# Projecting the context's first keys and values inside the first mixture of a transformer kernel, with a new order for the second stage

## Chip, cores and metric

The kernel runs on one core of a Trainium2 chip, in float32. The metric is the device time of one execution in microseconds (us); of several executions the median is taken. TensorE is called PE, VectorE DVE, ScalarE ACT, GpSimd POOL, SyncE SP, as in the profile.

## The reference, cut to what matters

Two blocks are applied to x (256 tokens of width 1024).

```python
x = x + token_mixer(rmsnorm(x))                # first block: 8 + 8 heads, forgetting and dilated attention
x = x + hierarchical_moe(rmsnorm(x))           # 32 experts, 1024 -> 512 -> 1024, two of them for each token
# second block, layer 0
h, hc = modulate(x, ...), modulate(ctx, ...)   # shifts, scales, gates: silu(c) @ ada_w, silu(c_ctx) @ ada_w
q, k, v, f = split(h @ attn_w_in)              # q, k, v of width 768, f of width 256
kc, vc = split(hc @ attn_w_in[:, 768:2304])    # keys and values of 256 context tokens
y = concat(diff_attend(q, [k, kc], [v, vc]), fourier_mix(f)) @ attn_w_out   # 6 differential heads
x = x + g_m * y
x = x + g_f * ec_moe(modulate(x, ...))         # 16 experts, 1024 -> 1024 -> 1024, 32 tokens for each expert
# layer 1: a gated short convolution in the place of attention, then a second ec_moe
```

Keys and queries are normalized for each head, multiplied by a gain, and turned by rope, but the context's keys get no rope. The context (hc, kc, vc) does not depend on x.

## The kernel before

**The ring.** All weights come through a ring of six slots of 2 MB (SLOTS = 6). plan_items lists the items in the order in which SP loads them. Before it issues item i, SP waits until item i - 6 has been released (load, free_main); it issues in order. A projection's item is released by its last matmul, a mixture's by M.done, a conditioning half ("ada") by its last addition. Two items of each mixture (LENT = 4 and 7) go into borrowed memory instead (arena from HEAD on, and gate_rows).

**The stages.** Stage 1 is norm, six projections with 16 attention heads in two token tiles between them, and the output projection; then routing (route1_dve, rank_pe) and the first mixture M1 with 32 experts. For each expert expert_pe does gate (L1461), turns the earlier expert's activation, up (L1461), the sums of four partial results (L1480), down of the expert before (L1511), and adds it back to the tokens (back_pe, L1537). For every fourth expert the tokens of four experts are gathered (L1379). Items of expert e in M1 are 3e - 1 (gate), 3e (up), 3e + 1 (down of e - 1). PE, ACT and DVE write out experts 0 to 3 and 28 to 31 and loop three times over eight experts; SP has a loop too. Then more_passes branches: only when an expert has more than 32 tokens is the whole mixture run again. close_y_pe (L1543) closes the sums.

**Stage 2** (block2_pe, block2_act, block2_dve, block2_pool) walks one list, steps2(), on every engine. A unit is one 128-token tile times 512 (wide) or 256 (narrow) columns of weights: projected on PE (proj_pe, L474), squared on ACT (L494), summed on DVE (L506), its root taken on POOL (L262), scaled and multiplied by the gain on DVE (L526, L532), with rope also by a rotation on POOL (L556) and an addition on DVE (L568), turned on PE (L586) and copied by ACT (L596). Values only need a copy. There are 18 units: context and own keys (4), queries (2), own and context values (4), the rest of queries and keys (2), of the context's keys (2), of the context's values and the own values (4). Between them stand attend2(s), the pipelined steps of 12 heads (scores L1952, maximum L1959, exponential L1967, mix L1976 to L1979, turn L1987, values L2012), and the conditioning: ada_add (L378, L384: DVE adds one eighth of a section of ada_w, weighted by silu(c)), ada_sum on PE (L397 to L404) and ada_use on DVE (L415 to L432). The context is normalized and turned in experts 28 to 30 of M1.

**Stage 3** is the convolution with its projections; the second and third mixtures follow the same scheme (16 experts, L1467 and L1511).

Of the kernel before, what the change touches and what calls it, by code (L numbers as in the profile page):

```python
# [9 lines left out]
ALU = mybir.AluOpType  # L10
# [21 lines left out]
LENT = (4, 7)  # L32
LAM_INIT = 0.8 - 0.6


class Mixture:
# [4 lines left out]
    def __init__(self, steps, ne, nf, nd, arrived, done, first, done0, k0, scale, shift, gate, fresh, stage):  # L41
        self.stage, self.lent = stage, LENT if stage else ()
        self.ne, self.nf, self.nd, self.per = ne, nf, nd, 2 * nf + nd
# [65 lines left out]
JOBS = [(s, c) for s in range(12) for c in range(2 if s < 2 else 1)]  # L109
ADDS = [(s, c, k) for s in range(12) for half in range(2) for c in range(2 if s < 2 else 1) for k in range(4 * half, 4 * half + 4)]  # L110
W_IN_COLS = {"qa": 0, "ka": 512, "va": 1024, "qb": 1536, "kb": 2048, "vb": 2560}
CHUNKS1 = ["qb", "kb", "vb", "qa", "ka", "va"]


def plan_items():
# [11 lines left out]
    after = [[], [(0, 0)], [], [(0, 1)], [(1, 0)], [(1, 1)]]  # L127
# [30 lines left out]
def transformer_blocks(nc, x, ctx_in, w_in, w_out, w_gate, w_up, w_down, ada_w, ada_b, attn_w_in, attn_w_out,  # L158
# [3 lines left out]
    with stack:  # L162
# [61 lines left out]
        for i in range(len(items)):  # L224
# [3 lines left out]
            if items[i][0] not in ("ada", "w_in", "attn_w_in", "attn_qk45", "w_out", "attn_w_out", "conv_w_out") or i == ITEM["proj2", 4]:  # L228
# [9 lines left out]
        chain_at = {"dve": 0, "act": 0, "pool": 0}  # L238
# [25 lines left out]
        def pool_step(ins):  # L264
            chain_at["pool"] += 1
            ins.then_inc(pool_chain, 1)
            nc.gpsimd.wait_ge(pool_chain, chain_at["pool"])

# [10 lines left out]
        def norm_act(j, src, i, ready):  # L279
# [6 lines left out]
            nc.scalar.activation(xn[:, 0, :], src[:, 0, :], ACT.Square, accum_out=ss[:, 0:1]).then_inc(sq_done[0], 1)  # L286
# [3 lines left out]
        def norm_dve(j, src, i, ready):  # L290
# [6 lines left out]
            nc.vector.tensor_tensor_reduce(out=xn[:, 1, :], in0=src[:, 1, :], in1=src[:, 1, :], scale=1.0, scalar=0.0,  # L297
# [4 lines left out]
        def norm_pool(j):  # L302

            for t in range(T):
                nc.gpsimd.wait_ge(sq_done[t], j + 1)
                pool_step(nc.gpsimd.tensor_scalar(ss[:, t:t + 1], ss[:, t:t + 1], 1.0 / D, EPS, ALU.mult, ALU.add))
# [51 lines left out]
        accs = {"own": ada_acc[:, :], "ctx": gate_rows[:, 1, 0, :], "even": arena[:, 10240:10240 + D], "odd": arena[:, HEAD:HEAD + D]}  # L358
        acc_of = ["own", "ctx", "own", "ctx", "even", "own", "even", "own", "even", "own", "odd", "own", "odd", "own"]
# [47 lines left out]
        def ada_use_dve(j, banks):  # L407
# [9 lines left out]
            if sec == G_M:  # L417
                g = gate_rows[:, l, 0, :]
# [17 lines left out]
        def heads(name, units, sq, qn, tmp, first_ready, banks):  # L436
# [152 lines left out]
            def put_act(u):  # L589
# [5 lines left out]
                for a, m, dst in un["put"]:  # L595
# [4 lines left out]
                        rope_dve=rope_dve, tr_pe=tr_heads_pe, put_act=put_act, put=put_, vput=vput, added=added,  # L600
# [266 lines left out]
        def turn_out1_pe(g):  # L867
# [4 lines left out]
            pe.wait_ge(ada_used, 2 if br else 4)  # L872
# [26 lines left out]
        def out1_pe(br, t, n):  # L899
# [6 lines left out]
            if br:  # L906
                for s_, v in h1["done"]:
                    pe.wait_ge(s_, v)
                if t:
                    pe.wait_ge(*((at_m, len(att1)) if n else (ada_used, 4)))  # L910
# [14 lines left out]
        CTX = E1 - 3  # L925
# [7 lines left out]
        def ctx_square_act():  # L933
            nc.scalar.wait_ge(ctx_loaded, 32)
            for t in range(T):
                nc.scalar.activation(ctx_junk, ctx_rows[t], ACT.Square, accum_out=ctx_ss[:, t:t + 1]).then_inc(ctx_sq, 1)
                nc.scalar.wait_ge(ctx_sq, t + 1)

        def ctx_root_pool():
            nc.gpsimd.wait_ge(ctx_sq, 2)  # L940
            pool_step(nc.gpsimd.tensor_scalar(ctx_ss, ctx_ss, 1.0 / D, EPS, ALU.mult, ALU.add))
# [7 lines left out]
        def ctx_turn_pe(t):  # L949
# [3 lines left out]
            pe.wait_ge(M1.act, CTX + t + 1)  # L953
# [14 lines left out]
        def ctx_put_dve(t):  # L968
            nc.vector.wait_ge(ctx_tr, 2 * t + 2)
            for k in range(4, KD):  # L970
# [6 lines left out]
                  22: [("ada_sum", 2)], 23: [("ada_use", 2), ("ada_sum", 3)], 24: [("ada_use", 3)],  # L977
# [3 lines left out]
        def attend1(s):  # L981
# [12 lines left out]
            if 18 <= s < 22:  # L994
                yield "ada_add", 1

        def steps1():
# [12 lines left out]
            for u in range(6, 12):  # L1010
# [16 lines left out]
                if u >= 10:  # L1027
# [1518 lines left out]
```

## Time and profile before

| | us |
|---|---|
| median of 3 runs (2025.22 to 2026.14) | 2025.56 |
| the profiled execution | 2021.36 |
| its span, first to last instruction | 2019.5 |
| PE busy | 1496.5 (74%) |
| DVE busy | 485.2 (24%) |
| ACT busy | 246.0 (12%) |
| POOL busy | 89.1 (4%) |
| bytes moved by DMA | 710.94 MB, 352 GB/s on average |

The span in 40 equal slices, busy share in tenths (9 is 90% or more; PEclk is the granted TensorE clock in tenths of full speed):

```text
PE   7999687777767698896765756655997766656665
DVE  3763321111111267743000000001653000000000
PEclk9989799989898899997887888778797887888778
DMA  9532599999999966445999999999893999999997
```

Rows of the windows view give for a stretch the busy us of each engine with the number of instructions, the granted clock (1.00 is 2.4 GHz), the DMA engines' mean busy share and GB/s. Rows of the timeline give start, length, engine, line of the kernel, operation, written and read names, shapes and the number of instructions merged; a bracket at the end gives the idle time of the engine before it and what ended it. A float32 matmul of the program shows as two MATMUL records.

### The profile page before, as it was taken

How to read it: one execution, taken by the hardware profiler on the slowest of the kernel's cores; microseconds unless marked ns; L12 is line 12 of the kernel's file. 1: busy time of each engine (PE TensorE's matmuls, PEld its weight loads, DVE VectorE, ACT ScalarE, POOL GpSimd, SP SyncE). 2: the span in 40 equal slices, each digit the busy share in tenths (PEclk: the TensorE clock that was granted, in tenths of full speed). 3: DMA queues.
4: the chain of work that ended last, by engine and by line, in shares of the span. 5: the costliest groups of instructions: out<-in, count | busy, mean ns of one | idle time of the engine just before them, and what ended most of it. 6: DMA issues, size and time to landing. Idle time of an engine off the chain costs nothing.

```text
span 2019.5 us, 28556 instructions
## 1 busy us (share of the span) xinstructions
PE 1496.5 (74%) x12460; PEld 838.8 (42%) x12460; DVE 485.2 (24%) x965; ACT 246.0 (12%) x603; POOL 89.1 (4%) x102
## 2 busy tenths in 40 slices
PE   7999687777767698896765756655997766656665
PEld 3455444433324344665432424222875432424222
DVE  3763321111111267743000000001653000000000
ACT  2122211111112111332000000001001000000000
POOL 2210000000000042100000000000000000000000
PEclk9989799989898899997887888787997887888778
DMA  9532599999999966445999999999893999999997
GB/s 360 194 140 74 219 405 423 420 422 423 420 423 421 406 252 237 188 163 198 426 419 419 422 421 419 422 421 403 339 372 127 418 419 422 421 420 420 422 420 321
DMA packets 118479, 710.94 MB, mean 352 GB/s; under 512 B 5856, under 2 KB 8416, under 8 KB 93664
## 3 DMA queue, kind: packets, MB, share of 16 engines
q1 hardware_dynamic: 117232, 706.95, 86.0%
q10 hardware_dynamic: 1136, 2.36, 0.3%
q8 instruction: 87, 1.43, 0.3%
q14 instruction: 24, 0.20, 0.0%
HBM read 708.25 MB, written 1.05 MB: 351 GB/s over the span
## 4 chain that ended last, share of the span: by engine, by line
DMA 55%; PE 31%; DVE 7%; issue 4%; POOL 2%; ACT 2%; SPq 0%; DVEq 0%; POOLq 0%; ACTq 0%
DMA ring<-in_moe_w_down 27%; DMA ring<-in_w_down 17%; DMA ring<-in_moe_w_up 11%; PE bank L1511 5%; PE bank L2309 4%; PE bank L474 4%; PE bank L1467 3%; PE bank L1379 3%; PE bank L914 1%; PE bank L618 1%; PE bank L2091 1%; POOL small L262 1%; PE bank L1461 1%; PE bank L1537 1%; DVE ada_acc L378 1%
## 5 line engine op out<-in xcount | busy, mean ns | idle before, releaser
L1467 PE MATMUL bank<-ring,arena 128*32 128x256 f32 x3968 | 286.7, 442 | 160.9 <-DMA ring<-in_moe_w_up 95.0
L1511 PE MATMUL bank<-ring,arena 128*32 128x256 f32 x3008 | 249.9, 490 | 186.6 <-DMA ring<-in_moe_w_down 140.9
L1467 PEld LDWEIGHTS bank<-ring,arena 128*32 128x32 f32 x3968 | 143.9, 123 | 285.2 <-issue 111.6
L1511 PEld LDWEIGHTS bank<-ring,arena 128*32 128x32 f32 x3008 | 119.7, 135 | 304.2 <-issue 193.7
L1461 PE MATMUL bank<-ring,arena 128*32 128x512 f32 x1024 | 136.2, 653 | 56.6 <-DMA ring<-in_w_up 36.8
L474 PE MATMUL bank<-ring,hT 128*128 128x512 f32 (+1 forms) x352 | 157.4, 599 | 1.6 <-DVE hT L336 1.6
L1583 DVE TENSOR_TENSOR arena<-arena,bank 128x128 f32<-128x128 f32 (+1 forms) x64 | 22.7, 355 | 499.0 <-PE bank L1467 496.7
L1379 PE MATMUL bank<-arena,xn 128*128 128x128 f32 x512 | 126.6, 410 | 3.3 <-DVE arena L1411 3.3
L1379 PEld LDWEIGHTS bank<-arena,xn 128*128 128x128 f32 x512 | 123.6, 336 | 8.0 <-issue 4.3
L1537 PE MATMUL bank<-arena 32*128 32x256 f32 x1024 | 95.7, 444 | 16.8 <-PE bank L1537 10.6
L474 PEld LDWEIGHTS bank<-ring,hT 128*128 128x128 f32 x352 | 67.7, 198 | 73.6 <-issue 70.8
L1589 ACT ACTIVATE arena<-bank 128x256 f32<-128x256 f32 x64 | 24.5, 383 | 549.8 <-PE bank L1524 546.7
L1598 DVE TENSOR_TENSOR arena<-bank,gate_strips 128x256 f32<-128x256 f32 x32 | 13.6, 425 | 308.8 <-PE bank L1511 308.8
L2309 PE MATMUL bank<-hT,ring 128*128 128x256 f32 x384 | 85.7, 386 | 1.5 <-ACT hT L328 1.5
L2309 PEld LDWEIGHTS bank<-hT,ring 128*128 128x128 f32 x384 | 74.4, 194 | 12.5 <-ACT hT L328 1.9
L1461 PEld LDWEIGHTS bank<-ring,arena 128*32 128x32 f32 x1024 | 29.9, 115 | 115.3 <-issue 90.5
L1558 DVE COPY arena<-bank 128x512 f32<-128x512 f32 x32 | 22.1, 691 | 211.6 <-PE bank L1461 211.6
L1537 PEld LDWEIGHTS bank<-arena 32*128 32x128 f32 x1024 | 41.8, 191 | 60.8 <-PE bank L1537 37.6
L378 DVE SCALAR_TENSOR_TENSOR ada_acc<-ring,condT,ada_acc 128x1024 f32<-128x1024 f32 x49 | 64.6, 1319 | 1.2
L262 POOL TENSOR_TENSOR small<-small,columns 128x8 f32<-128x8 f32 (+3 forms) x26 | 38.9, 1496 | 294.5 <-DVE small L252 220.2
L1565 ACT ACTIVATE arena<-bank 128x128 f32<-128x128 f32 (+1 forms) x64 | 21.0, 328 | 249.5 <-PE bank L1491 249.5
L1577 ACT ACTIVATE arena<-bank 128x128 f32<-128x128 f32 (+1 forms) x64 | 21.0, 328 | 240.0 <-PE bank L1480 233.2
(263 smaller groups left out, 1289.9 us busy)
## 6 DMA issues: line engine op xcount, KB each, us to landing
ring<-in_moe_w_down SPq DMA_DIRECT2D x64, 2048.0 KB, 26.5
ring<-in_moe_w_gate SPq DMA_DIRECT2D x62, 2048.0 KB, 24.8
ring<-in_moe_w_up SPq DMA_DIRECT2D x62, 2048.0 KB, 26.9
ring<-in_w_gate SPq DMA_DIRECT2D x32, 2048.0 KB, 25.2
ring<-in_w_up SPq DMA_DIRECT2D x32, 2048.0 KB, 26.1
ring<-in_w_down SPq DMA_DIRECT2D x30, 2048.0 KB, 26.5
ring<-in_ada_w SPq DMA_DIRECT2D x24, 2048.0 KB, 13.0
ring<-in_w_in SPq DMA_DIRECT2D x6, 2048.0 KB, 14.6
```

Of the source, the lines that this page charges most:

```text
L262: nc.gpsimd.tensor_tensor(dst, src, minus_half[:, 0:src.shape[1]], ALU.pow).then_inc(roots_done, 1)
L378: ins = dve.scalar_tensor_tensor(acc, w, by, acc, ALU.mult, ALU.add)
L474: last = nc.tensor.matmul(banks[u % NB][:, 0:n], un["lhs"][:, k, :], ring[un["item"] % SLOTS][:, k, a:a + n], start=(k == 0), stop=(k == K ...
L1379: last = nc.tensor.matmul(XG[kk % 4][:, 0:GE * C], xn[:, t, kk::KD], sel[:, b * T + t, :], start=(t == 0), stop=(t == T - 1))
L1461: last = nc.tensor.matmul(GU[up][32 * j:32 * j + 32, :], xgT[:, x + kk, a:a + C], w[:, kk, :], start=(kk < 4), stop=(kk >= 4))
L1467: last = nc.tensor.matmul(GU[up][32 * j:32 * j + 32, 0:QW], xgT[:, x + kk, a:a + C], w[:, kq, j * QW:(j + 1) * QW], start=(kk == 0), stop= ...
L1511: last = nc.tensor.matmul(z_bank(M)[32 * j:32 * j + 32, 0:QW], act_s[:, b, q * C:(q + 1) * C], w[:, kq, j * QW:(j + 1) * QW], start=(kk == ...
L1537: nc.tensor.matmul(Y[2 * t + j // 2][:, at:at + QW], wselT[rows_, e % 2, t * P:(t + 1) * P], z_s[rows_, :], start=(n == 0 and e == 0 and M ...
L1558: v.tensor_copy(up_s, GU[1][:, :]).then_inc(M.u_dve, 1)
L1583: nc.vector.tensor_tensor(silu_s[:, 0:M.w], silu_s[:, 0:M.w], gate_up(M)[1], ALU.mult).then_inc(M.act, 1)
L1589: nc.scalar.activation(wselT[:, e % 2, :], WT[:, 0:S], ACT.Copy).then_inc(M.wT, 1)
L2309: last = nc.tensor.matmul(odd_banks(i)[b // 2][:, (b % 2) * S:(b % 2 + 1) * S], ring[it % SLOTS][:, k, b * P:(b + 1) * P], hT[:, k, :], st ...
```

## The change

What it does, part by part:

1. **Guests.** The context's keys and values of the first four heads (columns 768 to 1279 and 1536 to 2047 of attn_w_in) are projected in M1, at the end of PE's steps of experts 24 and 28 (unit_pe). Their weights are two more items of the ring, placed ahead of the gate item of expert 24 (item 71) and of expert 28 (item 83). Squares, sums, roots, gains and transpositions of the two key tiles follow in experts 24 to 27. The context is loaded in expert 20 and turned in experts 21 and 23. The results stay in the upper arena (k_ctx) and in gate_rows (v_ctx).
2. **Loops.** PE, ACT and DVE loop twice instead of three times over eight experts and write out experts 20 to 31. SP writes out all experts.
3. **Stage 2** has 14 units: context keys and values of heads 4 and 5 first (a new item attn_45, columns 512 to 767 of keys and of values), then own keys, queries, values, the rest. Attention starts at unit 9, with two steps in each of units 9 to 11. The additions are spread anew. x is turned at units 2 and 3.
4. **Conditioning.** Section 3 moves from stage 2 to stage 1, with its two items, eight additions, its sum and its use.
5. **The branch** after M1 is written as a compare-and-branch with a hint, whose place is marked ahead of expert 28.
6. **Routing and norms.** In the first routing the ranking matmuls need only the two choices, not the gates, and the flag for more passes is computed after the first gather. In the other two routings one step is folded into a copy and a fill is moved ahead of a wait. In the norms the scale 1/D goes into the squaring instruction, and the added eps too for the second tile.
7. **Lending.** In stage 2 the first borrowed area is free when the last scores are done.

The diff, cut to its core:

```diff
+CTX_LOAD, CTX_TURN, UNITS, UNIT_TURN = 20, {21: 0, 23: 1}, {24: 0, 28: 1}, {25: 0, 27: 1}
+GUESTS = {3 * e - 1: g for e, g in UNITS.items()}
+SECTIONS = [0, 1, 3, 2, 4, 5, 6, 7, 8, 9, 10, 11]
-    after = [[], [(0, 0)], [], [(0, 1)], [(1, 0)], [(1, 1)]]
+    after = [[], [(0, 0)], [], [(0, 1)], [(1, 0), (1, 1)], [(3, 0), (3, 1)]]
-    items += [("moe", i) for i in range(3 * E1) if i not in LENT]
-    after = [[(2, 0), (2, 1)], [(3, 0)], [(3, 1), (4, 0), (4, 1), (5, 0)], [(5, 1), (6, 0), (6, 1)], [(7, 0), (7, 1)]]
-    for n, item in enumerate([("attn_w_in", 768), ("attn_w_in", 0), ("attn_w_in", 1536), ("attn_qk45",), ("attn_w_in", 2048)]):
+    for i in range(3 * E1):
+        if i in GUESTS:
+            at["guest", GUESTS[i]] = len(items)
+            items.append(("attn_w_in", (768, 1536)[GUESTS[i]]))
+        if i not in LENT:
+            items.append(("moe", i))
+    after = [[], [(2, 0)], [(2, 1), (4, 0)], [(4, 1)], [(5, 0), (5, 1)], [(6, 0), (6, 1), (7, 0), (7, 1)]]
+    for n, item in enumerate([("attn_45", 1), ("attn_w_in", 768), ("attn_w_in", 0), ("attn_w_in", 1536), ("attn_45", 0), ("attn_w_in", 2048)]):
...
+            released[ITEM["guest", g]] = (cu_mm, T * g + T)
+        def unit_pe(n, e):
+            pe.wait_ge(ctx_act, n % T + 1)
+            pe.wait_ge(ctx_dve, n % T + 1)
+            if n % T:
+                pe.wait_ge(M1.act, e + 1)
+            i = ITEM["guest", n // T]
+            wait_item(pe, i)
+            for k in range(KD):
+                last = nc.tensor.matmul(CT[t][:, :], ctxT[:, k, t * P:(t + 1) * P], ring[i % SLOTS][:, k, :], start=(k == 0), stop=(k == KD - 1))
+            last.then_inc(cu_mm, 1)
...
             if e:
                 back_pe(M, k, e - 1, r)
...
+            if M is M1 and e in UNITS:
+                for n in range(T):
+                    unit_pe(T * UNITS[e] + n, e)
+            if M is M1 and e in UNIT_TURN:
+                unit_turn_pe(UNIT_TURN[e], e)
...
             def put(i, rows_):
+                if i in M.guests:
+                    load_one(ITEM["guest", M.guests[i]])
                 free(M, k, i, r, looped)
...
-        LOOPS = E1 // (2 * GE) - 1
+        LOOPS = E1 // (2 * GE) - 2
...
-        def more_passes(eng, passes, one_pass, at_end=None):
-            with eng.If(passes > 0):
+        def more_passes(eng, passes, hint, one_pass, at_end=None):
+            name = f"more_passes_{eng.engine.name}"
+            eng.br_lt(passes, 1, on_true=name + "_none", on_false=name).branch_hint(hint)
...
-        for name, n, ctx in (("k", 0, 1), ("k", 0, 0), ("q", 1, 0), ("v", 2, 0), ("v", 2, 1), ("qk45", 3, 0), ("k45", 3, 1), ("v45", 4, 1),
-                             ("v45", 4, 0)):
+        for name, n, ctx in (("k45", 0, 1), ("v45", 0, 1), ("k", 1, 0), ("q", 2, 0), ("v", 3, 0), ("qk45", 4, 0), ("v45", 5, 0)):
...
-            for u in range(NU2):
+            for u in range(8):
+                yield "proj", (u, (0, 1))
+                if u == 7:
+                    yield "ada_sum", 5
+                if 2 <= u < 4:
+                    yield "turn_x", u - 2
+                yield "sum", u
+                if u == 7:
+                    yield "ada_use", 5
+                if u >= 2:
+                    yield "ada_add", 1
+                if u == 3:
+                    yield "lambda", 0
+                yield "rope", u - 1
+                yield "gain", u
+                if u >= 3:
+                    yield "ada_add", 1
+                if u >= 2:
+                    yield "tr", u - 2
+            for u in range(8, 14):
                 wide = u < 12
+                s = 2 * (u - 9) if wide else u - 6
                 yield "proj", (u, (0,) if wide else (0, 1))
+                if u in (9, 11):
+                    yield "ada_sum", u // 2 + 2
+                    yield "ada_use", u // 2 + 2
+                if u == 8:
+                    yield "tr", 6
+                yield "rope", u - 1
+                yield "tr", u - 1
+                if u > 8:
+                    yield from attend2(s)
+                yield "ada_add", 2 if wide else 1
                 if wide:
                     yield "proj", (u, (1,))
                 yield "sum", u
+                yield "ada_add", 1 if wide else 2
                 yield "gain", u
+                if wide and u > 8:
+                    yield from attend2(s + 1)
+                if wide:
+                    yield "ada_add", 2 if u == 8 else 1
             yield "fourier_proj", 0
+            yield "ada_sum", 8
+            yield "ada_use", 8
             yield from attend2(8)
-            yield "ada_add", 2
+            yield "ada_add", 3
             yield "fourier_proj", 1
             yield from attend2(9)
+            yield "ada_add", 3
             yield "fourier_first", 0
             yield "ada_sum", 9
```

## Rows read from the trace of the kernel before

**Rows 1.** Windows by stage: stage 1, first mixture, stage 2.

```profile
core 0: us, PE busy (x) PEld busy (x) DVE busy (x) ACT busy (x) POOL busy (x), PEclk, DMA share, GB/s
0.00:212.00 212.00, 187.78 (x634) 99.04 (x634) 111.31 (x241) 52.73 (x133) 31.96 (x34) 0.94 0.54 199
...
241.00:694.00 453.00, 343.95 (x3392) 175.08 (x3392) 70.90 (x153) 66.81 (x171) 2.46 (x12) 0.92 1.01 418
694.00:922.00 228.00, 199.34 (x741) 114.67 (x741) 144.84 (x231) 55.70 (x126) 50.39 (x46) 0.96 0.58 222
```

**Rows 2.** Chain of waits in order of time (start, us, what), first mixture, expert 24.

```profile
578.19 26.42 DMA ring<-in_w_down
```

**Rows 3.** Timeline of PE, first mixture, experts 24 and 25.

```profile
574.94 3.20 PE L1511 MATMUL bank<-ring,arena 128*32 128x256 f32 x32 [2.96 <-DMA ring<-in_w_down]
...
579.64 0.71 PE L1537 MATMUL bank<-arena 32*128 32x256 f32 x8 [0.17 <-PE bank L1537]
...
589.85 1.93 PE L1511 MATMUL bank<-ring,arena 128*32 128x256 f32 x32 [1.48 <-DMA ring<-in_w_down]
```

**Rows 4.** Transfers: L1724 from 110 to 215 us; the page's DMA issues.

```profile
DMA to landing us min/median/max: 7.7/7.8/9.1
...
ring<-in_w_down SPq DMA_DIRECT2D x30, 2048.0 KB, 26.5
```

**Rows 5.** Timeline of PE, stage 2: wide unit, transpositions, two narrow units' time.

```profile
712.63 7.03 PE L474 MATMUL bank<-ring,gate_rows 128*128 128x512 f32 x16
...
726.37 0.60 PE L586 MATMUL bank<-cb,arena 128*128 128x128 f32 x4
...
815.78 3.62 PE L474 MATMUL bank<-ring,gate_rows 128*128 128x256 f32 x16
```

**Rows 6.** Timeline of PE at the branch.

```profile
699.31 1.87 PE L1543 MATMUL bank<-columns 128*128 128x1 f32 x8 [5.51 <-issue]
701.04 8.50 PE L474 MATMUL bank<-ring,gate_rows 128*128 128x512 f32 x16
```

**Rows 7.** Timeline of PE, stage 2: the long gaps, the last conditioning sum.

```profile
752.78 0.66 PE L586 MATMUL bank<-cb,arena 128*128 128x128 f32 x4 [2.62 <-DVE gate_rows L421]
...
804.31 1.09 PE L586 MATMUL bank<-cb,arena 128*128 128x128 f32 x4 [5.77 <-issue]
...
830.76 0.69 PE L586 MATMUL bank<-cb,arena 128*128 128x128 f32 x2 [5.95 <-DVE gate_strips L415]
...
869.46 1.05 PE L404 MATMUL bank<-cb,ada_acc 128*128 128x128 f32 x8
```

**Rows 8.** Timeline of POOL, stage 2: root and rotation.

```profile
740.72 4.16 POOL L556 TENSOR_TENSOR arena<-arena,cb 128x128 f32<-128x128 f32 x4 [1.53 <-DVE arena L532]
745.04 2.06 POOL L262 TENSOR_TENSOR small<-small,columns 128x8 f32<-128x8 f32 x1 [0.15 <-DVE small L252]
748.63 3.62 POOL L556 TENSOR_TENSOR arena<-arena,cb 128x128 f32<-128x128 f32 x4 [1.53 <-DVE arena L532]
```

**Rows 9.** Timeline of DVE, stage 2: four additions, two maxima, one step of a mix.

```profile
761.96 5.24 DVE L378 SCALAR_TENSOR_TENSOR ada_acc<-ring,condT,ada_acc 128x1024 f32<-128x1024 f32 x4
...
827.99 1.28 DVE L1959 TENSOR_REDUCE small<-bank 128x1 f32<-128x512 f32 x2
...
829.62 0.75 DVE L1979 SCALAR_TENSOR_TENSOR cb<-cb,small 128x512 f32<-128x512 f32 x1
```

**Rows 10.** Timeline, first routing: first ranking matmul, end of the flag.

```profile
226.09 0.64 PE L1269 MATMUL bank<-arena,cb 128*128 128x32 f32 x2 [6.95 <-DVE arena L1248]
...
229.74 0.15 DVE L1258 CAST flag<-small 128x1 int32<-128x1 f32 x1
```

**Rows 11.** Timeline, end of stage 2: a norm's GpSimd step, a routing's last step.

```profile
920.29 0.19 POOL L306 TENSOR_SCALAR small<-small 128x1 f32<-128x1 f32 x1 [7.02 <-DVE small L297]
...
937.07 0.28 DVE L1302 TENSOR_SCALAR arena<-arena 16x256 f32<-16x256 f32 x1
```

**Rows 12.** Timeline, end of stage 1: the last conditioning sum and use.

```profile
166.20 1.13 PE L404 MATMUL bank<-cb,gate_rows 128*128 128x128 f32 x8 [1.90 <-DVE mod L432]
...
168.59 1.28 DVE L426 TENSOR_REDUCE mod_ctx<-bank 128x4 f32<-128x512 f32 x2
```

More of the change, by code:

```diff
@@ L227, in transformer_blocks @@
                 n_done = moe_from + items[i][1]
-            if items[i][0] not in ("ada", "w_in", "attn_w_in", "attn_qk45", "w_out", "attn_w_out", "conv_w_out") or i == ITEM["proj2", 4]:
+            if items[i][0] not in ("ada", "w_in", "attn_w_in", "attn_45", "w_out", "attn_w_out", "conv_w_out") or i == ITEM["proj2", 5]:
                 n_done += 1
@@ L1347, in ring_place @@
         def ring_place(M, i):
-            return M.first + i - sum(1 for n in M.lent if n < i)
+            return M.first + i - sum(1 for n in M.lent if n < i) + sum(1 for n in M.guests if n <= i)
         def wait_moe_item(pe, M, i, r, k):
@@ L1751, in free_in_pass, with load_one @@
-        def free_in_pass(M, k, i, r, looped):
-            at = ring_place(M, i) - SLOTS
-            last = i - SLOTS if looped else [n for n in range(i) if n not in M.lent and ring_place(M, n) == at][0]
-            nc.sync.wait_ge(M.done, nth(M, M.done0 + last + 1, M.per, r, k - M.k0))
+        def load_one(i):
+            sp, what, c = nc.sync, items[i][0], items[i][1]
+            slot = ring[i % SLOTS]
+            if i >= SLOTS:
+                sp.wait_ge(*released[i - SLOTS])
+            if what == "ada":
+                w = ada_w[c][:, items[i][2] * D:(items[i][2] + 1) * D].rearrange("(p k) n -> p k n", p=P)
+                dst, src = rows_of(M2[0], slot[:, :, :].rearrange("p a b -> p (a b)")), w[:, 4 * items[i][3]:4 * items[i][3] + 4, :]
+            elif what == "attn_45":
+                w = attn_w_in[0][:, c * AW:(c + 2) * AW].rearrange("(p k) (g c) -> p k g c", p=P, g=2)
+                dst, src = slot[:, :, :].rearrange("p k (g c) -> p k g c", g=2), w[:, :, :, NC:AW]
+            else:
+                big = {"w_in": w_in[0], "w_out": w_out[0], "attn_w_in": attn_w_in[0], "attn_w_out": attn_w_out[0],
+                       "conv_w_in": conv_w_in[0], "conv_w_out": conv_w_out[0]}
+                order = "(k p) n -> p k n" if what in ("w_out", "attn_w_out", "conv_w_out") else "(p k) n -> p k n"
+                dst, src = slot[:, :, :], big[what][:, c:c + NC].rearrange(order, p=P)
+            sp.dma_start(dst, src).then_inc(arrived[i % SLOTS], 16)
@@ L1757, in src1, with load, free_in_pass @@
+        def load(a, b):
+            for i in range(a, b):
+                load_one(i)
+        def pass_sp(M, k, src, free):
+            for e in range(M.ne + 1):
+                load_expert(M, k, e, 0, False, src, free)
+        def free_in_pass(M, k, i, r):
+            nc.sync.wait_ge(M.done, nth(M, M.done0 + i + 1 - SLOTS, M.per, r, k - M.k0))
         def src1(what, x, n):
@@ L2184, in block2_pe @@
                 elif what == "turn_x":
-                    for t in range(T):
-                        tr_pe(2, t, xn_ready(2, t), ZB)
+                    tr_pe(2, i, xn_ready(2, i), ZB)
                 elif what == "tr":
```

337 lines of the change are left out of this document (178 added, 159 removed).

## Prediction

> **What bounds the kernel now.** I read the windows by stage first [rows 1]. In the first mixture (241 to 694 us) the 16 DMA engines are busy the whole stretch at 418 GB/s; TensorE (PE) is not full. Between the mixtures (694 to 922) it is the other way round: DMA share 0.58, PE busy 199 of 228 us. The chain of waits says the same: one expert after another it goes from a down projection to the transfer of a later one [rows 2]; the down weights of successive experts land 589.85 - 574.94 = 14.91 us apart, 4.97 us for each 2 MB item. So a us of DMA added to the mixture is a us of kernel, PE work there costs nothing as long as it lets the DMA run, and in stage 2 PE work counts, unless another engine ends last. All weights after the stage wait for the first expert to free slots, so every shift of a stage passes to the end.
>
> **Guests: two more transfers.** attn_w_in's columns 768 and 1536 are now read twice: 2 x 4.97 = +9.9 us, where the DMA is the bound. (A third added item, attn_45 for the context, falls in stage 2, where the DMA has room and two ada halves have left.)
>
> **Guests: the slots they hold.** This is the step on which the forecast rests. The ring has six slots and SP issues in order. The guest of expert 24 stands ahead of items 71 to 75 (gate, up 24, down 23, gate, up 25); item 76 needs the guest's slot, and SP waits for it with everything behind. The guest lands at t. DMA has work until t + 5 x 4.97 = t + 24.9. PE uses the guest only at the end of expert 24's step: down 23 lands at t + 14.9, and from there to the last back-matmul is 5.4 us in the profile (574.94 to 579.64 + 0.71) [rows 3], 4.2 us for expert 25, where the clock is high; I take 4.9. Then two wide units follow. A wide unit is 16 matmul records, 7.03 us by itself, 6.87 in a row [rows 5]: 13.9. The slot is free at t + 33.7. A transfer issued to an empty queue lands 7.8 us later [rows 4]; with 0.1 for the handoff that is t + 41.6, where a full queue would have landed it at t + 29.8. The DMA loses 11.8 us; with the guest of expert 28, 23.6 in all. Bounds: 11.1 each (the step of 4.2) and 14.0 (first unit at 8.50 us, as after the branch [rows 6], and the step of 5.6). The median of 26.5 us from issue to landing [rows 4] shows the depth: five items. Gathers of 7.9 us cost nothing now for that reason, and the short guest steps of experts 25 and 27 (a transposition, two copies) neither. Below nothing is excluded: no engine can fetch item 76 before its slot is empty.
>
> **Stage 2: what goes.** Four wide units (context k and v) leave PE: 27.5 us; with them two groups of four transpositions (0.6 each [rows 5]), and one conditioning sum moves to stage 1 (1.1 [rows 12]). That is 29.8 us of PE. But waits grow. I walked the new order from the closing matmul (0) to the last conditioning sum, which now stands at 869.46 - 699.31 = 170.2 [rows 6, 7]. PE: closing, four narrow units at 3.46 (3.62 alone [rows 5]), x turned, four wide units, sum and transpositions, first half of unit 8: 52. Then it needs unit 7's keys or queries turned, with rope. GpSimd makes a root (2.06) and a rotation (4.16) for each of four units in a row, with VectorE's scaling between, and the next root waits for the rotation: 7.9 each [rows 8]. Unit 4 is projected at 25.4; unit 7's rope is done at 25.4 + 1.6 + 4 x 7.9 + 1.4 = 60. PE waits 7.5 us; before, two units of other work lay there. From 60 VectorE has: 29 of the 40 additions at 1.31 (four take 5.24): 38.0; maxima of ten heads at 1.28 and nine mixes at 1.3: 24.5 [rows 9]; two qk45 units, 7.6; three uses, 4; output sums, 1.8. That is 76, and 8 more of waits for roots and for PE, so the last addition is done at 144, and the sum waits for it. PE's own work to there is 115; it waits 29, against 18 now, most of it in three gaps of 2.6, 5.8 and 6.0 [rows 7]. After each long gap PE's records are longer at a lower granted clock (four transpositions 1.09 after the 5.77 us gap, 0.60 otherwise [rows 5, 7]); four long gaps, half of that hidden behind VectorE: +5. So the sum comes at 149.5: stage 2 gives 20.5 us. Bounds: 29.8 if waits don't grow, 12 if they grow by twice as much. Its weights are there in time: each item's slot is freed 15 us or more ahead of its use by the same walk. What follows the last sum is unchanged.
>
> **The branch.** PE issues nothing for 5.51 us between the last back-matmul and the closing matmul [rows 6], while nothing it waits for is open. The hint is to have the target's instructions at hand. I take 4.9 off, leaving 0.6; bounds 0 and 5.5. Code loading is told by the Trainium skill too: "Runtime: NRT & Kernel Launch", section Instruction fetch mechanics, says that a taken branch out of the loaded pages stalls for a fetch, and that prefetch is purely sequential. By that, a hint placed four experts ahead could keep nothing, and the stall would stay (a rival below); the gap agrees with the first half, and no row here shows the second.
>
> **Stage 1.** Section 3's eight additions, its sum and its use come here. The additions fill VectorE idle time (VectorE busy 111 of 212 us [rows 1]) but for one in unit 11, where VectorE is the late one: +1.3. The new sum must wait for the use of the one before: in the present order the last one waited 1.90 us and took 1.13 [rows 12]; the new one, after a use that runs 168.59 to 170.3, delays PE by 2.9. Together +4.2; bounds 0 (the later waits absorb it) and 7. The output weights come two items later in the ring; the DMA has room there (share 0.54 [rows 1]), and the slots they need (ka's and that of ada (1, 0)) are freed two units ahead of their use.
>
> **Routing and norms.** The ranking matmuls (226.09 to 228.5) now run beside the seven gate steps, and three flag steps (to 229.9) come after the gather [rows 10]: 1.8 + 0.7 = -2.5. In each of the two later routings the last step (0.28 [rows 11]) and a fill of like size leave the chain: -1.0. In four norms the second tile's GpSimd step goes, 0.27 with its handoff [rows 11]: -1.1. Together -4.6; bounds -5.5 and -2. SP's unrolled list and the shorter loop issue the same transfers in the same order: 0. The context's own 1 MB moves from expert 28 to 20, still in the mixture: 0. The 0.5 MB gate row is now loaded at unit 3, for a use at unit 7, 28 us later: 0.
>
> **Sum** against the profiled execution (span 2019.5, its time 2021.4): 9.9 + 23.6 - 20.5 - 4.9 + 4.2 - 4.6 = +7.7 us. The median of the runs shown is 2025.56, 4.2 above that execution; the difference is put on the median: 2033.3 us.
>
> **Rivals.**
> 1. Stage 2 gives the whole 29.8 us, because VectorE and GpSimd catch up. For it: VectorE is busy only 145 of 228 us [rows 1]. Against: the in-order walk above puts 76 us of its work into 84. It gives 2033.3 - 9.3 = 2024.0.
> 2. No hole: the DMA queue outlasts the guest, as it does a gather now. This would need PE's guest step to end within 25 us of the landing; the rows give 34. It gives 2033.3 - 23.6 = 2009.7, faster. The point from which it decides is the guest's release at t + 24.
> 3. Both are worse: a slow first unit in the mixture (2 x 2.2) and stage 2 giving 12: 2033.3 + 4.4 + 8.5 = 2046.2. For it: a clock that falls after every gap [rows 5, 7], and VectorE's additions in every step of the walk.
> 4. The hint does nothing, the 5.5 us gap stays, as the change doesn't do what it says: 2033.3 + 4.9 = 2038.2. The page named above is on its side.
>
> **How the numbers follow.** About 0.2%, 4 us, is what a measurement can tell from no change. Forecast 0.47, rival 1 0.18, rival 2 0.12, rival 3 0.10, rival 4 0.13. Faster by more than 4 us: rival 2 and a quarter of rival 1, 0.17. Within 4 us: the rest of rival 1 and the lower edge of the forecast, 0.22. Slower: 0.61. The range takes in rivals 1 and 4, half the spread to 3, and leaves out rival 2: 2021 to 2044.
>
> **What would show it.** Two stretches of about 12 us with the DMA share well under 1, just after the context units in experts 24 and 28; SP waiting there some 35 us for the unit matmuls; 23 us of PE waits ahead of unit 8's second half, of unit 11 and of the last conditioning sum. Right on the hint: a gap under 1 us before the closing matmul. Wrong, if the DMA share stays at 1 through experts 24 to 31 while the mixture grows by 10 us only, or if the last sum comes 25 us or more earlier than now.

## The result and the profile after

The changed kernel takes 2031.92 us (median of 14 runs, 2028.59 to 2038.3) against 2022.16 for the kernel before (14 runs beside it). The ratio is 1.0047, 95% interval 1.0036 to 1.0057: slower by 0.47%, 9.5 us. The profiled execution took 2033.48 us, its span is 2031.7, 12.2 above that of before.

The windows of the changed kernel, first mixture and stage 2 (columns as in [rows 1]):

```profile
core 0: us, PE busy (x) PEld busy (x) DVE busy (x) ACT busy (x) POOL busy (x), PEclk, DMA share, GB/s
239.00:723.00 484.00, 373.25 (x3395) 188.32 (x3398) 74.86 (x162) 71.42 (x177) 5.19 (x10) 0.92 0.95 392
723.00:929.00 206.00, 178.59 (x738) 105.47 (x730) 125.05 (x208) 53.26 (x123) 40.66 (x41) 0.92 0.65 244
```

Set them beside [rows 1]. In the first mixture the DMA share was 1.01 at 418 GB/s and is 0.95 at 392: the stage that DMA bounds has become longer by more than its extra bytes. Stage 2 has 20.8 us of PE work less and is 22 us shorter; its DMA share stays low (0.65, before 0.58). The DMA line of the page's 40 slices (tenths) shows the loss as two single 7s among the 9s, in the slices that begin at 559 and 660 us. (In the line PEclk shown above for the kernel before, the page has 8, 7 and 9 in slices 27 to 29.)

```profile
DMA  9542699999979796463999999999993999999997
```

To find where 12.2 us arise I took the same landmarks from PE's timeline in both kernels: the second group of router matmuls, the first gather, the last down projection of the first mixture, the closing matmul [rows 6], the last conditioning sum [rows 7], the last down of the second mixture, the third gather, the last down of all. Before:

```profile
215.54 3.60 PE L1201 MATMUL bank<-router_sb,hT 128*128 128x36 f32 x16 [1.55 <-DVE hT L336]
...
230.28 7.91 PE L1379 MATMUL bank<-arena,xn 128*128 128x128 f32 x32 [1.85 <-DVE arena L1411]
...
689.72 1.93 PE L1511 MATMUL bank<-ring,arena 128*32 128x256 f32 x32 [0.37 <-ACT arena L1565]
...
1395.46 2.44 PE L1511 MATMUL bank<-ring,arena 128*32 128x256 f32 x32 [3.10 <-DMA ring<-in_moe_w_down]
...
1553.10 7.90 PE L1379 MATMUL bank<-arena,xn 128*128 128x128 f32 x32 [0.74 <-DVE arena L1411]
...
2009.77 1.93 PE L1511 MATMUL bank<-ring,arena 128*32 128x256 f32 x32 [2.96 <-DMA ring<-in_moe_w_down]
```

The changed kernel:

```profile
220.26 3.60 PE L1269 MATMUL bank<-router_sb,hT 128*128 128x36 f32 x16 [1.55 <-DVE hT L342]
...
232.36 7.91 PE L1451 MATMUL bank<-arena,xn 128*128 128x128 f32 x32 [1.20 <-DVE arena L1483]
...
727.63 1.93 PE L1589 MATMUL bank<-ring,arena 128*32 128x256 f32 x32 [0.37 <-ACT arena L1643]
...
734.30 1.43 PE L1621 MATMUL bank<-columns 128*128 128x1 f32 x8 [2.59 <-issue]
...
881.41 1.94 PE L411 MATMUL bank<-cb,arena 128*128 128x128 f32 x8 [6.07 <-issue]
...
1407.40 1.93 PE L1589 MATMUL bank<-ring,arena 128*32 128x256 f32 x32 [1.79 <-DMA ring<-in_moe_w_down]
...
1562.40 7.91 PE L1451 MATMUL bank<-arena,xn 128*128 128x128 f32 x32 [0.74 <-DVE arena L1483]
...
2019.12 3.64 PE L1589 MATMUL bank<-ring,arena 128*32 128x256 f32 x32 [2.96 <-DMA ring<-in_moe_w_down]
```

Differences of neighbouring landmarks, changed less before:

| stretch | before, us | changed, us | difference | predicted |
|---|---|---|---|---|
| start to router matmuls | 215.54 | 220.26 | +4.7 | +4.2, less a norm's 0.3 |
| router matmuls to first gather | 14.74 | 12.10 | -2.6 | -2.5 |
| first gather to last down of the mixture | 459.44 | 495.27 | +35.8 | +33.5 |
| last down to closing matmul | 9.59 | 6.67 | -2.9 | -4.9 |
| closing matmul to last conditioning sum | 170.15 | 147.11 | -23.0 | -20.5 |
| last sum to last down of the second mixture | 526.00 | 525.99 | 0.0 | -0.8 |
| that to the third gather | 157.64 | 155.00 | -2.6 | -1.0 |
| third gather to last down of all | 456.67 | 456.72 | 0.0 | 0 |
| last down to the end of the span | 9.73 | 12.58 | +2.9 | 0 |

The last line is not of the change: the last matmuls of this execution fell at a lower granted clock (the last down took 3.64 us against 1.93, the two back-matmuls behind it 1.2 against 0.7 each). In some later executions below they are short, in some long, with the same instructions there. Without it the rest is +9.3 us, close to the 9.8 us by which the medians differ.

Each column is one execution, and a stretch with the same instructions differs from one execution to the next. From the start to the router matmuls the ten other kernels with the change's stage 1 (e1 to e6 and e9 to e12 below) take 216.3 to 221.5 us, and e7, with the stage 1 of the kernel before, takes 214.2 against its 215.5. So a difference of 1 us in this table means little unless other profiles repeat it.

The hole can be seen three times. First SP, whose timeline stops twice, for 31 and 32 us, between two neighbouring issues (start, us):

```profile
573.20 0.33 SPq L1827 DMA_DIRECT2D ring<-in_w_up  x1
604.76 0.38 SPq L1827 DMA_DIRECT2D ring<-in_w_down  x1
...
649.61 0.33 SPq L1827 DMA_DIRECT2D ring<-in_w_up  x1
682.34 0.38 SPq L1827 DMA_DIRECT2D ring<-in_w_down  x1
```

Then the chain of waits (start, us, what), in which the two units stand between two waits for transfers: SP issues the next item (604.76 above) when the units end (604.73), and PE then waits for the transfers behind it.

```profile
586.73 1.93 PE bank L1589 x32
...
590.80 13.93 PE bank L952 x32
604.73 1.48 PE bank L1535 x13
606.20 22.57 DMA ring<-in_w_down
```

Then the windows of 2 us: the DMA queue is dry while PE multiplies (share 0.00 in all four from 596 to 604).

```profile
596.00:598.00 2.00, 2.00 (x6) 0.93 (x5) 0.00 (x0) 0.10 (x1) 0.00 (x0) 1.00 0.00 0
...
602.00:604.00 2.00, 2.00 (x6) 0.94 (x5) 0.00 (x0) 0.00 (x0) 0.00 (x0) 1.00 0.00 0
...
608.00:610.00 2.00, 1.44 (x20) 0.39 (x12) 0.69 (x1) 0.00 (x0) 0.00 (x0) 1.00 0.96 369
```

Down 23 lands at 586.6, so the guest, three items ahead of it, at 571.7 = t. The slot is released at 604.7, t + 33.0 (forecast 33.7).

### The profile page after: what moved, and what is told of

It is laid out like the page before. It is cut to its first block, busy times and chain, and to the rows that moved or that the text cites. A ratio compares the mean times of both kernels' runs of the same rounds, so it can differ in the third digit from the quotient of the medians.

```text
span 2031.7 us, 28333 instructions
## 1 busy us (share of the span) xinstructions
PE 1508.7 (74%) x12460; PEld 844.9 (42%) x12460; DVE 482.2 (24%) x963; ACT 248.5 (12%) x605; POOL 82.1 (4%) x92
## 3 DMA queue, kind: packets, MB, share of 16 engines
HBM read 714.54 MB, written 1.05 MB: 352 GB/s over the span
## 4 chain that ended last, share of the span: by engine, by line
DMA 53%; PE 37%; DVE 4%; issue 3%; ACT 1%; POOL 1%; SPq 0%; DVEq 0%; POOLq 0%; ACTq 0%
DMA ring<-in_moe_w_down 27%; DMA ring<-in_w_down 16%; DMA ring<-in_moe_w_up 10%; PE bank L481 7%; PE bank L1589 6%; PE bank L2442 4%; PE bank L1451 3%; PE bank L1541 3%; PE bank L921 1%; PE bank L952 1%; PE bank L2211 1%; PE bank L1535 1%; PE bank L1615 1%; PE bank L2073 1%; PE bank L625 1%
## 5 line engine op out<-in xcount | busy, mean ns | idle before, releaser
L1661 DVE TENSOR_TENSOR arena<-arena,bank 128x128 f32<-128x128 f32 (+1 forms) x64 | 22.7, 355 | 503.1 <-PE bank L1541 499.6
L385 DVE SCALAR_TENSOR_TENSOR ada_acc<-ring,condT,ada_acc 128x1024 f32<-128x1024 f32 x42 | 55.0, 1309 | 1.0
## 6 DMA issues: line engine op xcount, KB each, us to landing
ring<-in_ada_w SPq DMA_DIRECT2D x24, 2048.0 KB, 13.2
```

Of the source, the lines that this page charges most:

```text
L385: ins = dve.scalar_tensor_tensor(acc, w, by, acc, ALU.mult, ALU.add)
L1661: nc.vector.tensor_tensor(silu_s[:, 0:M.w], silu_s[:, 0:M.w], gate_up(M)[1], ALU.mult).then_inc(M.act, 1)
```

## The experiments

Spans of the profiled executions are beside the ratios, which are always against the kernel before.

**1. Is the loss the slot, or the work in itself?** Three kernels differ from the changed one only in where the guest stands in the queue. All three have the same bytes, the same instructions and the same order on PE.

```diff
-GUESTS = {3 * e - 1: g for e, g in UNITS.items()}   # changed kernel
+GUESTS = {3 * e + 2: g for e, g in UNITS.items()}   # e1, behind down 23
+GUESTS = {3 * e + 1: g for e, g in UNITS.items()}   # e2, ahead of down 23
+GUESTS = {3 * e: g for e, g in UNITS.items()}       # e3, ahead of up 24
```

> The changed kernel, but each guest stands three items later in the queue, behind down 23 (down 27), so that TensorE comes to it as soon as it lands. Hole theory: the guest lands at t, the two units end at t + 14, inside the 25 us of transfers behind it; no DMA hole, SP never waits over 15 us there. The first mixture takes 10 us more than before instead of 36 and the whole 24 to 26 us less than the changed kernel: about 2006 to 2008, ratio about 0.993. Rival (the two units are simply 28 us of TensorE work in a stretch that cannot carry it): time as the changed kernel's, 2032, with PE busy and no DMA room regained.

> The changed kernel, but each guest stands two items later, just ahead of down 23 (down 27). Hole theory: release at t + 5 + 4.9 + 13.9 = t + 23.8, landing of the next item at t + 31.7 against t + 29.8: a hole of 2 us each, 4 in all, so 4 above the run with the guest behind the down weights: 2011. Rival (TensorE work in itself): no difference from the changed kernel.

> The changed kernel, but each guest stands one item later, between gate 24 and up 24 (28). Hole theory: release at t + 28.7, hole 6.9 us each, 13.8 in all: 2021 to 2022, half way between. A step of 5 us for each item and guest. Rival (TensorE work in itself): no difference from the changed kernel.

| kernel | ratio, interval | span | first gather to last down | against e1 | expected |
|---|---|---|---|---|---|
| e1, behind down 23 | 0.9896, 0.9861 to 0.9931 | 2006.7 | 472.6 | 0 | 0 |
| e2, one item earlier | 0.9946, 0.9928 to 0.9964 | 2011.4 | 478.1 | +5.5 | +4 |
| e3, two earlier | 0.9985, 0.9970 to 1.0001 | 2020.6 | 486.1 | +13.5 | +13.8 |
| changed, three earlier | 1.0047, 1.0036 to 1.0057 | 2031.7 | 495.3 | +22.7 | +23.6 |

This is the dose that the slot theory asked for; the rival, PE work in itself, asked for no difference. In e1 SP still waits up to 17 us between two issues there (584.46 to 601.52; under 15 was expected), without a loss. PE's timeline shows the pair of units right behind the landing, and the windows show DMA at full share beside it (compare 590 to 610 with the dry windows above):

```profile
587.52 13.97 PE L952 MATMUL bank<-ring,gate_rows 128*128 128x512 f32 x32 [1.31 <-DMA ring<-in_attn_w_in]
```

```profile
590.00:600.00 10.00, 10.00 (x24) 4.38 (x23) 0.86 (x2) 1.23 (x2) 1.64 (x1) 1.00 1.01 416
600.00:610.00 10.00, 9.38 (x103) 3.70 (x101) 2.56 (x6) 2.02 (x5) 0.00 (x0) 1.00 1.01 425
```

So the 14 us of each pair of units are hidden, if the slot isn't held while PE does other things first. What is left in e1 against the kernel before is 472.6 - 459.4 = 13.2 us for two transfers (expected 10). In the profiles further below the same stretch takes 461.0 and 459.1 without guests (e7, e8) and 471.5, 472.0, 470.8 and 471.5 with them behind the down weights (e9 to e12). So it is 12 us for the two on the mean, 10 to 13.5 between single profiles. In these five kernels PE waits seven times for a guest, and each wait gives the distance from the down weights' landing to the guest's: 5.3 or 5.4 us six times, 6.6 once, against 4.97 for the mixture's own items. Two of e9's rows:

```profile
647.50 1.93 PE L1589 MATMUL bank<-ring,arena 128*32 128x256 f32 x32 [1.12 <-DMA ring<-in_w_down]
...
652.78 13.97 PE L952 MATMUL bank<-ring,gate_rows 128*128 128x512 f32 x32 [1.21 <-DMA ring<-in_attn_w_in]
```

That is 0.7 to 0.8 us of the 2 above 9.9 in the usual case; where the rest comes from wasn't tried.

**2. Does VectorE set stage 2?**

```diff
-ins = dve.scalar_tensor_tensor(acc, w, by, acc, ALU.mult, ALU.add)
+n = NC // 2 if sec in (2, 4, 5, 6, 7) else D
+ins = dve.scalar_tensor_tensor(acc[:, 0:n], w[:, 0:n], by, acc[:, 0:n], ALU.mult, ALU.add)
```

> The changed kernel, with the conditioning additions of stage 2 (sections 2, 4 to 7) done over 256 of 1024 columns behind their first; the rest of these sums is left out. If VectorE sets stage 2, as the prediction said: 29 shorter additions by about 0.9 us are 26 us of VectorE work less, and the waits of 4.3, 4.7 and 6.1 us ahead of unit 11's sum, unit 11's transposition and the last sum shrink to 5 us in all, the last sum comes 8 to 12 us earlier, the kernel 8 to 12 us faster than the changed one. If the waits are the chain of GpSimd's roots and rotations: under 3 us.

The kernel leaves out three quarters of these additions' columns. Ratio 0.9992 (0.9977 to 1.0007), which is 11 us below the changed kernel; from the closing matmul (734.77) to the last sum (871.37) it is 136.6 us against 147.1. In the chain of waits of the changed kernel the four gaps of PE in stage 2 are

```profile
790.35 2.62 issue
...
823.41 4.32 issue
...
844.35 4.73 issue
...
875.35 6.07 issue
```

and with the short additions the first is 1.02 us and the last three are 8.2 us instead of 15.1:

```profile
820.67 2.55 issue
...
840.32 3.12 issue
...
868.88 2.49 issue
```

The effect has the size that was expected (8 to 12 us), though the last three waits shrank by 7 us and not by 10: 1.6 came from the first, the other 1.9 mostly from records behind shorter gaps, which are shorter (the last sum's 1.94 us in the changed kernel is 1.74). The edit is not pure, though. GpSimd's root takes 2.60 us in the changed kernel, with an addition of 1.28 us beside it on VectorE, and 1.80 us here beside one of 0.48, so 0.8 us of each of the two waits at unit 11 can come through GpSimd. The last wait has no such doubt. VectorE's last three additions in the changed kernel are

```profile
877.39 3.92 DVE L385 SCALAR_TENSOR_TENSOR arena<-ring,condT,arena 128x1024 f32<-128x1024 f32 x3
```

They end at 881.31, and PE's sum starts at 881.41; with the short additions the same two times are 871.27 and 871.37. So VectorE sets the last sum. The first wait is another one: its transposition starts 0.1 us behind an addition of VectorE (792.18 to 792.87) that had itself waited for GpSimd's rotation.

**3. What is the hint worth, and when?** Two kernels undo or move it, one has it alone.

```diff
# e5: no mark, no hint; the branch has the new form
-eng.br_lt(passes, 1, on_true=name + "_none", on_false=name).branch_hint(hint)
+eng.br_lt(passes, 1, on_true=name + "_none", on_false=name)
# e6: the mark at the last expert
-if M is M1 and e == M.ne - GE:
-    loaded += [load_passes(eng), eng.mark_branch_hint_location()]
+if M is M1 and e == M.ne - GE:
+    loaded.append(load_passes(eng))
+if M is M1 and e == M.ne - 1:
+    loaded.append(eng.mark_branch_hint_location())
# e7: the kernel before, with the new more_passes and the marks as in the change
```

> The changed kernel without the hint and the marks: the branch itself is as in the changed kernel. If the hint gave the 2.9 us by which the gap before the closing matmul shrank (5.51 to 2.59): gap 5.5, the kernel 3 us slower. If the gap shrank because of the new form of the branch or the shape of the code: gap 2.6, no difference.

> The changed kernel with the mark of TensorE, VectorE and ScalarE one expert ahead of the branch instead of four. If what is fetched by the hint is partly lost over four experts of code: gap 0.6 to 1, 2 us faster. If the fetch only begins late or covers a part in any case: gap 2.6, no difference. If the mark comes too late: a gap over 2.6.

> The kernel before with the hinted branch alone. If the hint is worth what the gap showed: gap before the closing matmul 2.6 instead of 5.51, 2.9 us faster than before, ratio 0.9986. By my prediction it was 4.9 us: 0.9976.

The closing matmul in PE's timeline (its gap in brackets): without the hint (e5),

```profile
737.29 1.87 PE L1621 MATMUL bank<-columns 128*128 128x1 f32 x8 [5.63 <-issue]
```

with the mark one expert ahead (e6),

```profile
737.10 1.86 PE L1621 MATMUL bank<-columns 128*128 128x1 f32 x8 [3.10 <-issue]
```

and in the kernel before with the hint alone (e7), first PE, then VectorE's first instruction behind its own branch:

```profile
693.33 0.71 PE L1537 MATMUL bank<-arena 32*128 32x256 f32 x8 [0.16 <-PE bank L1537]
693.97 1.05 PE L1543 MATMUL bank<-columns 128*128 128x1 f32 x8
```

```profile
697.60 2.48 DVE L1608 TENSOR_TENSOR h<-h,bank 128x512 f32<-128x512 f32 x4 [5.21 <-issue]
```

The ratios are 1.0055 (1.0037 to 1.0072) for e5, 1.0051 (1.0035 to 1.0068) for e6 and 0.9964 (0.9949 to 0.9979) for e7. The times of e5 and e6 can't be told from the changed kernel's (1.0036 to 1.0057), so for them the gap decides. It says that the hint itself does it, not the form of the branch: 5.63 us without the hint, 2.59 with it and 2.55 to 3.10 in the nine other kernels built on the changed one that keep it. And its worth depends on the program it stands in: in the kernel before it takes the whole gap, and since PE doesn't rest, the closing matmuls take 1.05 us instead of 1.87; the kernel gains 7 us (4 to 10), 5.9 in span, 5.6 of it between the last down and the closing matmul (4.00 us against 9.59). My expectation for e7, 2.9, was too low, and 4.9, the forecast, was about right for that kernel and wrong for the changed one. VectorE, with the same hint, still shows 5.21 us for which the profile has no cause. What it would be without the hint can't be read, since in the kernel before VectorE waits for the closing matmul (7.79 us in all). It does not count, since PE has context units to do before it needs anything of h.

Why half of it stays in the changed kernel is not settled. The place of the mark isn't the reason (e6: 3.10, at the upper end of what the others show). To try the place of the target, two kernels on top of e1 put 18 or 36 matmuls in the part of the program that is skipped:

```diff
+if eng.engine == nc.tensor.engine:
+    for _ in range(36):        # 18 in e9
+        nc.tensor.matmul(bank[0][:, 0:P], ident, ident, start=True, stop=True)
 eng.br(name + "_none")
```

> The kernel with the guests behind the down weights, with 18 matmuls (72 instructions of TensorE's program) in the part that the branch skips: they never run, they move the branch's target by 72 instructions. In the kernel before with the hint alone the gap before the closing matmul was 0, in the changed kernel 2.6, with the guests last 2.9. If the place of the target decides what the hint keeps, the gap changes here or in the run with 144, to under 1 us, and the kernel is 2 to 4 us faster. If something else does (the longer program between mark and target): gap 2.6 to 3.1 in both.

> The same with 36 matmuls, 144 instructions, which puts the target at the same distance from a multiple of 256 as in the kernel before with the hint (146 there, 147 here; 3 in the changed kernel). If the place of the target decides: gap 0, 3 to 5 us faster than with the guests last alone, about 2002. If not: gap 2.9, 2006.

```profile
712.10 1.87 PE L1621 MATMUL bank<-columns 128*128 128x1 f32 x8 [2.93 <-issue]
```

```profile
707.30 1.36 PE L1621 MATMUL bank<-columns 128*128 128x1 f32 x8 [2.87 <-issue]
```

2.93 and 2.87 us (e9, e10), as the 2.87 of e1; ratios 0.9928 (0.9912 to 0.9943) and 0.9932 (0.9917 to 0.9947), which overlap e1's interval (0.9861 to 0.9931). The target's place isn't the reason either. One difference that remains between e7 and the others is the length of TensorE's program between mark and target, 4,507 instructions in e7 and 6,318 in the changed kernel (counted in the compiled programs); the e6 run, whose mark stands nearer, speaks rather against that too. It stays open.

**4. Routing and norms alone**, in the kernel before:

> The kernel before with the routing and norm edits alone. Prediction: 4.6 us faster (2.5 at the first routing, 1.0 in the two later ones, 1.1 in the norms), ratio 0.9977. If the steps only wait for something else: under 2 us, ratio above 0.999.

The edit is the change's own: `taken` computed ahead of the gate steps, `flag_dve` behind the gather, `aff_steps` with one step folded into a copy and the fill moved ahead of a wait, and the norm's factor in the square. Ratio 0.9968 (0.9956 to 0.9980), 6.5 us faster by the medians' ratio, 4.1 in span. The first gather stands at

```profile
227.22 7.91 PE L1386 MATMUL bank<-arena,xn 128*128 128x128 f32 x32 [1.20 <-DVE arena L1418]
```

against 230.28, 3.1 us earlier: 2.65 of them lie behind the router matmuls (215.13 here), as predicted (2.5). The other 0.4 can't be given to the first norm: e7, without these edits, is 1.3 earlier there. Between the second mixture and the third gather e8 takes 155.0 us and e7 156.0, with the same time for the last down: 1.0, as predicted for routing and norm there. The span's 4.1 agrees with the 4.6 predicted; the interval (4.0 to 8.9 us) holds both.

**5. A version that beats both.** Stage 2's additions keep their order, but two more are made at unit 1, where VectorE still waits for others, and two fewer ahead of the last sum. It stands on e1; e12 is the same with e10's skipped matmuls.

```diff
                 yield "gain", u
+                if u == 1:
+                    yield "ada_add", 2
...
             yield from attend2(9)
-            yield "ada_add", 3
+            yield "ada_add", 1
```

> The kernel with the guests behind the down weights; of stage 2's 40 additions the order is kept, but two are made more at unit 1, where VectorE still has idle time, so that two fewer are left ahead of the last conditioning sum. If VectorE sets the last sum: 2.6 us less wait there (6.1 to 3.5), the kernel 2 to 3 us faster than with the guests last alone: span 2004. If not: no difference, 2006.7.

> Guests behind the down weights, two additions earlier, target of the branch moved by 144 instructions. If both hold they add: 2000 to 2002, ratio about 0.990 or lower. If neither: 2006.

In e11 PE's wait for the last sum is 3.35 us instead of 6.07:

```profile
852.33 1.94 PE L411 MATMUL bank<-cb,arena 128*128 128x128 f32 x8 [3.35 <-issue]
```

That is the 2.7 us by which VectorE was relieved (two additions of 1.3), and a second sign that VectorE sets it, with nothing left out of the sums. Ratios: e11 0.9908 (0.9892 to 0.9923), median 2003.04 us; e12 0.9896 (0.9880 to 0.9913), median 1999.45 us. Between the two there is no difference that the intervals can tell, and e12's skipped matmuls gave nothing at the branch (its gap is 3.09 us). e12 differs from e10 (0.9917 to 0.9947) in the two additions alone, and there the intervals are apart: 7 us by the ratios, where 2 to 3 were expected. e11 against e1 (0.9861 to 0.9931) shows nothing, as e1's interval is the widest. Both are 1% faster than the kernel before, and 1.4 to 1.5% faster than the change as it was.

## Why the prediction was right, point by point

The forecast of 2033.3 us stands 1.4 above the measured median, and its sign (slower, 0.61) was right. That it is so near is in part luck. The sum was put on a median of 2025.56 us, of three runs; the fourteen runs beside the changed kernel have 2022.16. Between like and like the forecast is +7.7 and the measured +9.5 (by the ratio) or +9.8 (by the medians). And the terms' errors offset each other in part: too little slowdown in the mixture (2.3 us) and in stage 1 (0.8), too much gain at the branch (2.0) and behind stage 2 (0.8), against too little gain in stage 2 (2.5) and ahead of the third gather (1.6). Two sums of the prediction don't close: 144 and 5 are 149, not 149.5, and 170.2 less 149.5 is 20.7, not 20.5. This changes nothing.

- **The slots (+23.6): right in mechanism and size.** The three queue positions give 22.7 for the whole. The release was forecast at t + 33.7 and came at t + 33.0, since the step ahead of the units took 4.2 us and not 4.9; the pair of units took 13.93 against 13.9. Down 24 was due 14.9 us behind down 23's landing at 586.6 and is used at 612.87, 26.1 behind it: 11.2 to the first landing, 11.8 forecast. Another 1 us (down 25 is used 16.0 us behind down 24, not 14.9) is lost afterwards, while the queue fills again. The second hole shows the same: 11.2, then 1.0.
- **The two transfers (+9.9): too small.** The kernels without a hole show 12 (10 to 13.5). This term, not the hole, is what the mixture's +35.8 against +33.5 comes from. I had priced them by the landing distance of the mixture's own weights, and had no row for such a transfer in a full queue.
- **Stage 2 (-20.5): right in mechanism, at least 2.5 too small.** The pair of profiles gives -23.0. The same stretch takes 170.2 to 173.5 us in three profiles with the old stage 2 (before, e7, e8) and 145.4 to 147.4 in eight with the new one (changed, e1 to e3, e5, e6, e9, e10), which is 25 on the mean. VectorE ends last, as e4 and e11 show. The single waits were not right. The one for unit 7's transposition, forecast at 7.5, took 2.62: PE came to it 56 us behind the closing matmul (790.35 - 734.30), not 52, and went on at 58.7, not 60. Of the 4 us, 3 are the first three narrow units, which took 13.45 us and not 10.4, at a granted clock of 0.78 (window 735.7 to 749.1). The waits at unit 11 are 4.32 and 4.73, the one for the last sum 6.07: 17.7 us in all, where 23 were forecast. VectorE's last addition ends 147.0 us behind the closing matmul, 3 later than the 144 forecast, and the sum starts 0.1 behind it. So the 5 us for a lower clock, which the forecast put on top of VectorE's end, are not a term of their own. The clock does fall behind gaps: the last sum took 1.94 us, in the kernel before 1.05 [rows 7], and the transpositions behind the gap of 2.62 us 1.09, not 0.60 [rows 5]. But that is inside VectorE's time, which waits for PE in places. Rival 1 (the whole 29.8) is reached by no pair of these profiles (the widest is 28.1), and the waits that it left out are there. But the mean of 25 lies midway between it and the forecast, and touches the prediction's own sign of being wrong, a last sum 25 us or more earlier.
- **The branch (-4.9): the weakest step.** It gave 2.9. That the hint shortens the gap is shown by e5 and e7; that the gap is the fetch of the target's instructions agrees with them, but no row here shows the fetch. The size was taken as if a hint gave all or nothing. The gap was to be under 1 us and is 2.59. The rival that the hint does nothing (2038.2) fell: 5.63 us without it, 2.59 with it. The rule behind that rival is of the Trainium skill, "Runtime: NRT & Kernel Launch", section Instruction fetch mechanics: a taken branch out of the loaded pages stalls for a fetch, and prefetch is purely sequential. The first half agrees with the gaps of 5.51 and 5.63 us. The second would leave the gap whole, and in e7, with the mark four experts ahead, nothing of it was left.
- **Stage 1 (+4.2): about right, its terms less so.** +4.7 up to the router matmuls. The new sum with its wait took 3.7 (1.75 and 1.94; 2.9 forecast), and VectorE delays PE by 0.7 more at unit 11 (1.3 forecast). The half unit behind the new sum took 6.20 us against 4.82, which the sum didn't have. About 1.0 came back in the second tile of the norm, where the transpositions took 1.16 us against 1.90. Such shifts of the clock differ between executions.
- **Routing and norms (-4.6): right in sum.** First routing -2.6 (2.5 forecast). Between the second mixture and the third gather 2.6 us went, against 1.0 forecast; but 1.6 of it is the clock at the end of the mixture, in this pair of executions: the last down took 1.93 us against 2.44, and the two back-matmuls behind it 0.71 each against 1.24 and 1.23. Between e7 and e8, where these are alike, it is the 1.0 that was forecast.
- **Rival 2 (no hole, 2009.7)** was the right description of the kernel one gets when the guest stands three items later: e1's median is 2005.31, and its point of decision, a release at t + 24, is the position of e2, with a loss of 2 to 3 us for each guest.

## What to carry to other kernels

In a kernel that streams weights through a ring, the cost of an extra item is its transfer and the time that its slot is held: compute the time from landing to release against what is queued behind it, and place the load just ahead of its use, not ahead of work that comes first on the same engine. A change with several parts can lose by one of them alone: here a position in a list, three items off, turned a gain of 14 to 21 us (e9, e10 and e1) into a loss of 9.5. And where an engine ends last by a queue of small steps, look for its idle time early in the stage before removing anything: two additions earlier shortened PE's wait by 2.7 us.

## What the runs showed of the hardware that was not expected

- The same branch hint took away all of a 5.5 us gap in one program (e7: 0.0) and half of it in ten others (2.55 to 3.10 us), whatever the place of the mark or the target.
- Where the hint took away TensorE's gap (e7), VectorE's first instruction behind its own branch still came 5.21 us after its last one. Whether the hint did anything for VectorE isn't shown.
- When a DMA queue of 16 engines had run dry, the loss was more than the distance to the next landing: 11.2 us to the first, and 1 us more up to the landing three items on, at both holes.
- Two added transfers of 2 MB, of 512 columns each out of a wider matrix, took 12 us (10 to 13.5) in a stream where the others take 4.97 each; six of seven such transfers landed 5.3 to 5.4 us behind the one before. What makes them slower isn't known.
- GpSimd's root over 128x8 took 2.60 us with a full addition of VectorE beside it (1.28 us) and 1.80 us with a short one (0.48 us, e4); its rotation in units 4 and 5 took 3.18 and 2.38.
